# Down projection of a SwiGLU block by seven half-width products instead of eight

## What is computed

```python
hf = rms_norm(x, ln_ffn_pre[l])
g = jnp.einsum("bsd,df->bsf", hf, w_gate[l])
up = jnp.einsum("bsd,df->bsf", hf, w_up[l])
ff = jnp.einsum("bsf,fd->bsd", jax.nn.silu(g) * up, w_down[l])
x = x + rms_norm(ff, ln_ffn_post[l])
```

## Time and profile before

| | before |
|---|---|
| median of 3 runs | 2499.32 us (2498.97 to 2500.64) |
| profiled execution, its own time | 2498.34 us |
| its span on the slowest core | 2496.8 us |
| matrix engine (PE) busy | 97% |
| weight loads (PEld) busy | 44% |
| VectorE (DVE) busy | 43% |
| ScalarE (ACT) busy | 26% |
| granted TensorE clock, mean over the core | 0.990 |

### The profile page before, as it was taken

One profiled execution on the slowest core, in us unless ns is written; L12 is line 12 of the kernel. 1 busy time (PEld: TensorE's weight loads), 2 busy tenths in 40 slices (PEclk: granted clock), 3 DMA queues, 4 the chain that ended last, 5 costly groups with the idle time before them and its releaser, 6 DMA issues.

```text
span 2496.8 us, 31889 instructions; the slowest of 8 cores (2491.2 to 2496.8 us)
## 1 busy us (share of the span) xinstructions
PE 2431.3 (97%) x11547; PEld 1102.5 (44%) x11547; DVE 1061.8 (43%) x1622; ACT 640.5 (26%) x1184; POOL 210.3 (8%) x363
## 2 busy tenths in 40 slices
PE   5999999999999999999999999999999999999996
PEld 2444444444444444444444444444444444444442
DVE  3456537455454553321235552655545454300113
ACT  3332334122222222311123333432222222111111
POOL 0000000000000000002101000000000000000111
PEclk8999999999999999999999999999999999999998
DMA  8979868989989998767987524897445444344763
GB/s 208 182 102 137 169 223 173 185 123 135 133 129 132 133 130 235 255 208 195 253 146 110 96 80 169 226 191 122 85 89 91 91 85 85 114 158 151 222 195 97
DMA packets 76058, 377.14 MB, mean 151 GB/s; under 512 B 8320, under 2 KB 10624, under 8 KB 46592
## 3 DMA queue, kind: packets, MB, share of 16 engines
q0 software_dynamic: 52720, 310.93, 63.4%
q1 hardware_dynamic: 23184, 64.19, 8.2%
HBM read 512.44 MB, written 65.01 MB: 231 GB/s over the span
## 4 chain that ended last, share of the span: by engine, by line
PE 94%; DMA 3%; DVE 2%; issue 0%; SPq 0%; ACT 0%; DVEq 0%; ACTq 0%; POOLq 0%
PE bank L409 92%; DMA unit<-wst_gu 2%; DMA F<-xt 1%; PE bank L606 1%; PE bank L449 1%; PE bank L878 1%; DMA unit<-wst_in 0%; DVE XG L444 0%; DVE unit L441 0%; DVE F L441 0%; PE bank L401 0%; DVE XG L441 0%; SPq L505 0%; PE bank L537 0%; DVE F L444 0%
## 5 line engine op out<-in xcount | busy, mean ns | idle before, releaser
L409 PE MATMUL bank<-XG,unit 128*128 128x512 bf16 x7680 | 1679.7, 380 | 13.0 <-DMA unit<-wst_in 7.0
L409 PEld LDWEIGHTS bank<-XG,unit 128*128 128x128 bf16 x7680 | 752.0, 98 | 924.7 <-issue 24.3
L409 PE MATMUL bank<-F,unit 128*128 128x512 bf16 x3072 | 669.2, 379 | 0.0
L409 PEld LDWEIGHTS bank<-F,unit 128*128 128x128 bf16 x3072 | 300.6, 98 | 362.5
L441 DVE TENSOR_TENSOR tt<-tt 128x512 f32<-128x512 f32 (+1 forms) x151 | 104.1, 691 | 592.1 <-ACT tt L438 575.2
L435 ACT ACTIVATE tt<-bank 128x512 f32<-128x512 f32 x228 | 136.2, 597 | 481.2 <-PE bank L409 474.5
L441 DVE TENSOR_TENSOR bank<-bank,tt 128x512 f32<-128x512 f32 x152 | 106.3, 699 | 356.4 <-PE bank L409 356.4
L438 ACT ACTIVATE tt<-bank 128x512 bf16<-128x512 f32 (+1 forms) x160 | 95.0, 596 | 486.8 <-PE bank L409 481.2
L441 DVE TENSOR_TENSOR unit<-unit 128x1024 bf16<-128x1024 bf16 x304 | 196.1, 686 | 10.0 <-PE bank L409 2.1
L441 DVE TENSOR_TENSOR F<-bank,tt 128x512 bf16<-128x512 f32 x138 | 95.2, 691 | 120.1 <-PE bank L409 98.8
L357 POOL DMA_DIRECT2D unit<-wst_gu x100 | 52.9, 529 | 1017.7 <-PE bank L409 913.8
(11 more groups left out here) (72 smaller groups left out, 860.5 us busy)
## 6 DMA issues: line engine op xcount, KB each, us to landing
unit<-wst_gu POOLq DMA_DIRECT2D x100, 1024.0 KB, 10.8
unit<-wd_bf POOLq DMA_DIRECT2D x64, 1024.0 KB, 5.9
unit<-wo_bf POOLq DMA_DIRECT2D x32, 1024.0 KB, 6.0
unit<-wst_in POOLq DMA_DIRECT2D x31, 1024.0 KB, 13.8
unit<-wd_bf POOLq DMA_DIRECT2D x32, 768.0 KB, 7.3
wd_bf<-wst_dn POOLq DMA_DIRECT2D x32, 704.0 KB, 16.6
tt<-xt SPq DMA_DIRECT2D x64, 256.0 KB, 6.2
yT<-XG POOLq DMA_DIRECT2D x50, 256.0 KB, 9.6
```

Source lines behind the costliest of these rows:

```text
L409: inst = e.matmul(out, lhsT=pairs[n][0], rhs=pairs[n][1], start=(start and n == 0), stop=(stop and n == nk - 1), skip_group_check=lax)
```

## The change

The down stage is written anew. Of the 44 contraction blocks, 32 (in the first stage 16) are done in seven products for eight, over the two 256-token halves of the tile: two halves of the tokens, two halves of each group of 16 contraction blocks, two output tiles. Each product is a run of 8 matmuls (16 where two groups are used) of 256 tokens. The other 12 (28) contraction blocks are plain, now also in 256-token pieces. So a matmul has 256 columns where it had 512. In the names of the code: `nS` is the number of groups of 16 in seven products, `quad` a quarter of a weight unit, `sums` the three sums of quarters that are made for a block (S1 and S2 outside the ring, in `SQ`, one of them in place), `Tb` the three tables of sums of token blocks (`T`), made once per stage by `tsum`, with a fourth made in place in F0 or F1. `snap` copies a bank out while it is still being accumulated into (three times in a block), so the next product into that bank waits for the copy.

The weights in `wd_bf` are stored in another order, on the host. The side work is laid out anew: in the first stage eight chunks of x at a time are squared in blocks 1 to 4, and `side` now stands between the last but one and the last run of a block; the 32 scalings of chunks all lie in the second stage, four in every block (`nx_to`). The squares of the output are now taken from the finished tile in SBUF. `load_pw` comes after the second stage. `ffb` places the output tiles of the odd token tile in another order, and `TAIL_ORDER` follows it.

```diff
+            if par:
+                return (F0, "F0", 2 * i) if i < 4 else (XG, "X", 24 + 2 * i)
+            return XG, "X", 32 + 2 * i if i < 12 else 2 * i
...
         def dn_tile(par, side, apart=False):
+            p = cur["p"]
             acc = Acc(KC, apart=apart)
-            pend = []
+            Fp = (F0, F1)[par]
+            nS = 1 if (p, par) == (0, 0) else 2
+            US = range(nS)
...
+            def sums(s, u):
+                S1, K1 = SQ(u, 0)
+                S2, K2 = SQ(u, 1)
+                tt(S1, quad(s, 2), quad(s, 3), ALU.add, [("U", s, 2), ("U", s, 3)], K1)
+                tt(S2, S1, quad(s, 0), ALU.subtract, K1 + [("U", s, 0)], K2)
+                tt(quad(s, 2), quad(s, 0), quad(s, 2), ALU.subtract, [("U", s, 0), ("U", s, 2)], [("U", s, 2)])
+
+            def prod(bank, lhs, rhs, start):
+                for u in US:
+                    l, kl = lhs(u)
+                    r, kr = rhs(u)
+                    mm_group(bank, lambda k: l[:, k * 128:(k + 1) * 128], lambda k: r[:, k, :], range(8),
+                             reads=kl + kr, ncols=HT, start=start and u == 0, lax=not (start and u == 0))
...
+            nun = [use_unit("dn") for _ in US]
+            for u in US:
+                sums(slot_of[nun[u]], u)
+            tsum(T(0), B(0, 1), B(0, 0))
+            tsum(T(1), B(1, 1), T(0))
             for c2 in range(8):
-                bb = [next_bank(), next_bank()]
-                for ch in range(3):
-                    un = use_unit("dn")
-                    s = slot_of[un]
-                    ks = list(range(16 * ch, min(FC, 16 * ch + 16)))
-                    w = units[s][:, 0:len(ks) * 256].rearrange("p (k n) -> p k n", n=256)
-                    for e2 in range(2):
-                        mm_group(bb[e2], lambda k: w[:, k - 16 * ch, e2 * 128:(e2 + 1) * 128], lambda k: ffa(par, k), ks,
-                                 reads=[Kffa(par, k) for k in ks] + KU(s), start=(ch == 0), stop=(ch == 2))
...
+                if first:
+                    c, d = next_bank(), next_bank()
+                    if nS == 1:
+                        plain_q(d, slot_of[u1], 16, 1, 1, True)
+                        plain_q(c, slot_of[u1], 16, 0, 0, True)
+                    else:
+                        u2 = use_unit("dn")
+                        tail_d(True)
+                        tail_c(True)
+                a = next_bank()
+                prod(a, Q(ss, 0), B(0, 0), True)
+                s1 = snap(0, a)
+                for u in US:
+                    tt(quad(ss[u], 0), quad(ss[u], 1), SQ(u, 1)[0], ALU.subtract, [("U", ss[u], 1)] + SQ(u, 1)[1], [("U", ss[u], 0)])
+                if first:
+                    tsum(B(0, 1), B(1, 1), B(0, 1))
+                    tsum(T(2), B(1, 0), T(1))
+                elif nS == 1:
+                    d = next_bank()
+                    plain_q(d, slot_of[u1], 16, 1, 1, True)
+                else:
+                    c = next_bank()
+                    prod(c, Q(ss, 1), B(1, 0), True)
+                b = next_bank()
+                prod(b, lambda u: SQ(u, 0), T(0), True)
+                s5 = snap(1, b)
+                prod(a, lambda u: SQ(u, 1), T(1), False)
+                h2 = snap(2, a)
...
+                prod(b, Q(ss, 0), B(1, 1), False)
+                prod(a, Q(ss, 2), B(0, 1), False)
+                tt(snv[1], banks[a.i][:, 0:HT], snv[1], ALU.add, [a, s5, h9], [s5])
...
+                prod(a, Q(ss, 3), T(2), False)
+                done(*un)
...
+                if c2 < 7:
+                    nun = [use_unit("dn") for _ in US]
+                    sums(slot_of[nun[0]], 0)
...
+                if c2 < 7 and nS == 2:
+                    sums(slot_of[nun[1]], 1)
+                tt(o1[:, HT:TT], banks[d.i][:, 0:HT], snv[1], ALU.add, [d, s5, h9], k1)
+                plain(b, slot_of[u2], 32, 12, 0, 1, False)
+                tt(o0[:, HT:TT], banks[b.i][:, 0:HT], snv[2], ALU.add, [b, h2], k0)
                 side(c2)
...
+                plain(a, slot_of[u2], 32, 12, 1, 0, False)
+                done(u2)
+                act_copy(o1[:, 0:HT], banks[a.i][:, 0:HT], [a], k1)
+                for o, k in ((o0, k0), (o1, k1)):
+                    acc.square(o, k)
+                    acc.add()
             return acc
...
+            def nx_to(c2):
+                par = c2 // 4
+                for k, (v, keys) in enumerate(nx["bufs"], 4 * (c2 % 4)):
+                    stt(xg(par, k), v, C_G0 + k, Tt[par][:], keys + [rsp[2 + par]], [Kxg(par, k)])
...
+                if 1 <= c2 <= 4:
...
+                    for v, keys in nx["bufs"]:
+                        a2.square(v, keys)
                         a2.add()
-                        nx_load()
```

More of the change, by code:

```diff
@@ L1103, in dn_tile @@
[L1103 to L1110 removed]
+            Fp = (F0, F1)[par]
+            nS = 1 if (p, par) == (0, 0) else 2
+            US = range(nS)
+            h9 = P.alloc("t", 9)
+            first_use = {0: [h9], 1: [h9], 2: ["xhalo"]}
+            snv = (Tt[9][:, 0:HT], Tt[9][:, HT:TT], xhalo[:].rearrange("p a b -> p (a b)"))
@@ new lines, in Bq, with quad @@
+            def Bq(h, half, u):
+                o = 16 * u + 8 * h
+                return Fp[:, o:o + 8, half * HT:(half + 1) * HT], [Kffa(par, o + i) for i in range(8)]
+            def quad(s, n):
+                return units[s][:, 1024 * n:1024 * n + 1024]
+            def sums(s, u):
[4 more added lines that the diff above has]
+                tt(quad(s, 2), quad(s, 0), quad(s, 2), ALU.subtract, [("U", s, 0), ("U", s, 2)], [("U", s, 2)])
@@ new lines, in prod, with Q, plain_q @@
+            def prod(bank, lhs, rhs, start):
[4 more added lines that the diff above has]
+                             reads=kl + kr, ncols=HT, start=start and u == 0, lax=not (start and u == 0))
+            def Q(ss, n):
+                return lambda u: (quad(ss[u], n), [("U", ss[u], n)])
+            def plain_q(bank, s, k0, e2, half, start):
+                mm_group(bank, lambda k: gq(s, e2, k), lambda k: Fp[:, k0 + k, half * HT:(half + 1) * HT], range(16),
+                         reads=[Kffa(par, k0 + k) for k in range(16)] + KU(s), ncols=HT, start=start, lax=not start)
@@ new lines, in plain, with snap @@
+            def plain(bank, s, k0, nk, e2, half, start):
+                w = units[s][:, 0:nk * 256].rearrange("p (k n) -> p k n", n=256)
+                mm_group(bank, lambda k: w[:, k, e2 * 128:(e2 + 1) * 128],
+                         lambda k: Fp[:, k0 + k, half * HT:(half + 1) * HT], range(nk),
+                         reads=[Kffa(par, k0 + k) for k in range(nk)] + KU(s), ncols=HT, start=start, lax=not start)
+            def snap(n, bank):
+                h = P.alloc("sn", n)
+                extra = first_use.pop(n, [])
+                rd = [h9] if n < 2 and not extra else []
+                act_copy(snv[n], banks[bank.i][:, 0:HT], [bank] + rd, [h] + extra)
+                return h
@@ new lines, in T, with tsum, B @@
+            def T(n):
+                return lambda u: Tb(n, u)
+            def tsum(out, a, b):
+                for u in US:
+                    o, ko = out(u)
+                    x, kx = a(u)
+                    y, ky = b(u)
+                    tt(o, x, y, ALU.subtract, kx + ky, ko)
+            def B(h, half):
+                return lambda u: Bq(h, half, u)
+            nun = [use_unit("dn") for _ in US]
+            for u in US:
+                sums(slot_of[nun[u]], u)
+            tsum(T(0), B(0, 1), B(0, 0))
@@ L1281, in side_d1 @@
                               f"xl{n}", reads=[("y", to, 2 * n), ("y", to, 2 * n + 1)], writes=Kx2(n))
[L1282 to L1291 removed]
+                if p == 0:
+                    nx_to(c2)
             acc = dn_tile(1, side_d1, p == 1)
+            if p == 0:
+                load_pw()
             tail = Tail(to, acc)
```

152 lines of the change are left out of this document (88 added, 64 removed).

## The result

| | before | after |
|---|---|---|
| median of 5 runs | 2499.32 us (2498.10 to 2841.62) | 2521.66 us (2517.96 to 2967.71) |
| ratio of after to before | | 1.0082 [1.0062, 1.0102] |
| span, slowest core | 2496.8 us (core 1) | 2518.8 us (core 6) |

The change made the kernel slower by 0.8%: 20.5 us by the ratio, 22.3 by the medians, 22.0 by the spans, where 2497 was forecast and 2518 was the upper end of the range.

A forecast was written before the change was run, and what follows sets the result against it. PE was taken to bound the kernel, busy 97% of the span. Terms: -41.4 + 13.7 + 4.7 + 10.2 + 6.0 + 1.0 + 3.4 = -2.4 us, so 2497 against the median 2499.3; range 2472 to 2518.

The forecast's parts named there:

- Clock: Granted clock falls behind PE waits at the fourth block's end and third stage's start, 1.7 us each: +3.4 us.
- the waits of 3.8: Starts of the second and fourth stage: one PE wait of 3.8 us in each, on VectorE.
- Rival 2: Clock also falls behind 2.0 us waits and fully behind those of 3.8: 7 x 1.7 = 11.9 us, 2509; chance 0.22.
- In `load_pw` and the new order of outputs I see no cost: Pooling weights are wanted two and a half mixing steps later, output buffers freed as early as before: no cost.
- Columns removed: Down stages: 5184 matmuls of 256 columns at 109.3 ns, 566.6 us instead of 608.0: 41.4 us saved.
- Side work in the first stage: PE waits for `snap` behind ScalarE's squares and for VectorE's sum: 2.6 us in three blocks, 5.9 in the fourth, +13.7.
- Side work in the second stage: VectorE's scalings, adds and quarter sum make PE wait 0.9 us in three blocks and 2.0 in another: +4.7.
- Starts: Stage starts: second and fourth 5.1 us late each on VectorE, first and third 2.0 and 4.0 on data: 10.2 and 6.0.
- End: Last bank copy and a square stand ahead of the last square: +1.0 us.
- What would show it: Signs: 109 ns runs, named PE waits, PEclk under 1.00 behind them; down stages 605.6 us, wrong if under 592.
- Rival 1: Waits do not form, since squares run ahead and PE's lead covers the side; only starts and end count: 2475, chance 0.25.

The follow-up runs named there:

- last_scale: The changed kernel with the last block's four chunk scalings issued behind the second stage's last adds; 2513.03 us, ratio 1.0063 to the kernel before.
- later_slots_gate: later_slots with eight 512 KB loads of x held until the first mixing output is written; 2475.26 us, ratio 0.9903 to the kernel before.
- slots: The changed kernel with the ring buffer that gu_fast frees last taken fourth, not first, at a pair's down-stage start; 2514.60 us, ratio 1.0055 to before.
- early_sums: later_slots_gate with weight sums for the second and fourth stages' first block made in the preceding stage's last block; 2468.96 us, ratio 0.9879 to before.
- pair1_only: Seven products in the third and fourth stage only, the first two with the down stages of before; 2490.09 us, ratio 0.9955 to before.
- later_slots: The changed kernel with side work issued inside the next block, plus the buffer order of slots; 2479.73 us, ratio 0.9936 to before.

## Why the prediction was wrong

It named the right places for the waits in the down stages, and their sum, and still missed the time by 24 us. Two steps failed.

**"Clock."** It gave the falls 3.4 us: two of them, 1.7 each. On the slowest core there were seven in the down stages, behind its seven waits of 2.46 to 4.95 us, and the 10-us rows show 1.5 to 3.2 us lost behind each, 15.7 in all. So most of the miss is the count, five more falls at 1.7, and 3.8 us are the size, 2.2 for 1.7. The words "behind the waits of 3.8 PE waits for VectorE anyway" were wrong: behind 3.63 at the second stage's start the next wait was 0.6 us, 23 us later. The two rows that I took the price from, waits of 2.1 and 2.3, could give no limit either: waits of 2.1 to 2.7 have a fall behind them on one core and none on another. Rival 2, "slower, by the clock", had the mechanism and its seven falls, with up to 5 us for late transfers, and 2509 to 2514; it had 0.22, and set its price at the same 1.7.

**"In `load_pw` and the new order of outputs I see no cost."** The step looked at the pooling weights and at the output buffers, and left out the third thing that moved: the chunk loads, from a ring that ran ahead to groups of four whose buffers come free by scaling. The wait of 8.16 and the clock behind it, 9.3 us in the balance of that stretch, stood in no term and in no rival; rival 2 had late chunks, but ahead of VectorE's sums in the second stage. last_scale and later_slots_gate show that it hangs on transfers: order alone moves it to the third mixing step, holding back the eight big loads removes it.

By its own steps:
- Columns removed: right, 109.3 forecast, 109.2 and 109.3 measured. The Trainium skill, "TensorE: Matmul & The Clock Gate", section "Back-to-back issue gap", also has a formula for the gap of an isolated matmul, from which an estimate of 109.2 ns at 256 columns follows; the traces agree with it, and in sustained streams at that.
- Side work in the first stage: right in kind, ScalarE's queue ahead of `snap`. 13.7 forecast, 10.0 measured (1.06, 0.29, 2.28, 4.39, 1.93): the wait behind the table load was 4.4 for 5.9.
- Side work in the second stage: wrong in kind. "Weight sums of the next block (six of 0.69) fill VectorE until the block's end, so the side starts at 0" fails in three blocks: they wait for the second unit, which POOL issues behind the side's own DMAs and which lands 14 to 15 us after that. 4.7 forecast, 10.3 measured. I had said of a moved step that its queues count, and did not follow POOL's.
- Starts: 16.2 forecast, 14.7 measured; right, with 1.3 us more for the first and third and 3.1 less for the others. slots and early_sums take most of them away.
- End: 1.0 forecast, 1.3 measured. (Under "What would show it" the forecast's 605.6 for the down stages counts this 1.0 in; without it the terms give 604.6, and 619.9 was measured.)

Rival 1, that the waits don't form, had 2475. later_slots_gate came to that (2475.26) once the side work and the loads stood elsewhere: VectorE and ScalarE had the time, the order didn't give it to them. That the two numbers meet is in part chance, since later_slots_gate also has less waiting at the starts than rival 1 counted.

What stays open: why the third stage's start waited 5.6 us for its units in pair1_only and 2.7 on this core of after; why the transfers, and with them the entry wait, differ so much from core to core; and how much of the circle of the second stage is POOL's order and how much the slow landing. No run changed the clock by itself: its price is read from the rows.

## What to carry to other kernels

Where fewer columns shorten a bound engine's work, work out for each engine in strict order what stands ahead of the one instruction that it waits for, the queues that issue DMAs included, and put side work behind that instruction: here this was worth 31 us, where the columns saved 42. To each wait of some 3 us or more on the matrix engine add 1.3 to 3.2 us for the clock, as all 42 such waits here had it, and give waits of 2.1 to 2.7 us an even chance of it. Where the time is that of the slowest core, look at the others too: here the mean core lost 13.6 us and the slowest 22. A load that nobody needs soon can be the cause of a wait: gating eight of them on a later event gave 8 us, 6 either way.

## What the runs showed of the hardware that I had not expected

- The clock's price does not follow the length of the wait: on core 6 the 10-us stretches lost 1.7 us behind 2.46 and behind 2.68, 3.2 behind 3.16, 1.5 behind 4.06, 3.0 behind 4.95 and 2.0 behind 8.16. The same instruction's wait of 2.28 us had a fall behind it on seven cores and none on the eighth.
- With DMA shares of 0.97 to 1.05 a load of 256 KB took 27.8 us to land, and the loads of 512 KB were slower still: in later_slots, issued from 1242.7 on, their median was 37.1 with one chunk counted in, in later_slots_gate, issued from 1277.6 on, 10.2.
- Splitting a product of 512 columns into two of 256, each with a weight load of its own, costs 1.3%: 146.88 us for 145.04.
